# The mLSTM value projection taken two panels at a time, with 512 moving weight columns

## The chip, the cores and the metric

One core of a Trainium2 chip runs the whole kernel. The metric is the device time of one execution in microseconds (us); the median of three runs of the kernel before is 1903.33 us (1903.31 to 1904.78). All arithmetic is in float32; the large matrix products are made of three products of values rounded to fp32r (see below), so that a product of two float32 matrices costs three passes of TensorE.

## The reference, cut to what matters

Two layers of a parallel-branch block over 256 latent tokens and 256 context tokens, D_MODEL 1024. Per layer:

```
h = adaLN(RMSNorm(x))
parts = h @ w_in          # mLSTM q, k, v, o-gate, gates; GQA q, k, v; conv u, B, C; 3 merge gates
mlstm: 4 heads, q and k 128 wide, v 256 wide, both directions, context state first
    num = sum_s (q k^T * w_intra) v + ... ; den = row sum of the same weights
    h_out = num / max(|den|, exp(-m))
ym = h_out * rsqrt(mean h_out^2) * gain * sigmoid(o)
merged = sum_b sigmoid(gate_b) * (y_b @ P_b);   x += g1 * (merged @ w_out)
x += g2 * (relu(adaLN(RMSNorm(x)) @ w_up)^2 @ w_down)
```

The change concerns `v`, the third part: for 512 tokens and 4 heads of 256 columns it is h (512 x 1024) times 1024 columns of w_in.

## The kernel before, in words

**Panels.** All weights are cut into panels of 1024 rows and 256 columns (1 MB each). A layer has 90 of them, numbered through both layers by p; in layer 0 the panels 0 and 1 are mLSTM k (mk), 2 and 3 are q (mq), 4 to 7 are v (mv, one panel for each head, c = 0 to 3), 8 to 11 are the o-gate (mo). Layer 1 has the same at 90 and up, so its value panels are 94 to 97. A panel goes through these steps:
- SyncE loads it by one DMA into a buffer of `raw`, which has RAW = 4 places, place p % 4 (`load_panel`, L902). The load waits until panel p - 4 has been multiplied (L939).
- ScalarE rounds it to fp32r into `wH` (L1297, two instructions of 128x1024), which has HIGH = 3 places, place p % 3. It waits until panel p - 3 has been multiplied (L1295), because that panel's weights lie in the same place.
- VectorE subtracts: `wL` = raw - wH (L1697, two instructions), written over the raw values.
- TensorE multiplies (`run_panel`) and adds three products for each tile of 128 rows of the contraction (8 tiles, kt): high x high, high x low and low x high. Its last matmul increments the semaphore panel_done.
- ScalarE or VectorE takes the result out of one of the two PSUM slots (p % 2), and slot_free allows panel p + 2.

Two panels ahead: in the step of panel p, ScalarE and VectorE first split panel p + 2 (AHEAD = 2), and only then take the result of panel p out.

**Order of the work.** `make_plan` writes one list of steps, and each engine walks through it in order and does its own part of each step; semaphores join the engines. Around the value panels the list says: mq 1, gate_scan (VectorE), mv 0, gate_e, mv 1, gate_e2, mv 2, gate_cols (32 small transposing matmuls on TensorE, L1149), mv 3, then for head 0: weigh (TensorE L1162 and L1169, ScalarE exponentials L1512 into EP, VectorE L2011, GpSimd's triangular mask L1658), the o-gate panel mo 0 on TensorE beside that, and value (TensorE L1193), which needs the mask, the products and the head's values in `vaug`.

**The value panels.** For most panels the weights are the stationary operand and 512 tokens (256 in layer 1 where only latent tokens count) are the moving one. For the mv panels it is the other way round, as the result must have the tokens on the partitions: 128 tokens of h are loaded as the stationary operand and the 256 columns of the panel's weights move. So each mv panel has 4 token tiles x 8 kt x 3 products = 96 matmuls with 256 moving columns (L986 to L988). VectorE copies the result into `vaug` (L1753), and `mv_ready` counts one for each panel; value of head h waits for h + 1 of the layer.

Of the kernel before, what the change touches and what calls it, by code (L numbers as in the profile page):

```python
# [20 lines left out]
F32 = mybir.dt.float32  # L21
# [5 lines left out]
P = 128  # L27
# [505 lines left out]
def trunk(nc, x, c, ctx_in, c_ctx, w_ada, b_ada, norm1, norm2, w_in, gate_b, mnorm, qnorm, knorm, conv_w,  # L533
          w_pm, w_pa, w_pc, w_out, w_up, w_down, fnorm, consts, out):
    ctx = ExitStack()
    with ctx:
# [8 lines left out]
        xT = at("xT", [P, KT, TOK], F32, o); o += K16  # L545
        hH = at("hH", [P, KT, TOK], F32R, o); o += K16
        hL = at("hL", [P, KT, TOK], F32R, o); o += K16
        raw = at("raw", [P, RAW, KT, PC], F32, o); o += RAW * KT * PC * 4
        wL = at("wL", [P, RAW, KT, PC], F32R, o - RAW * KT * PC * 4)
        wH = at("wH", [P, HIGH, KT, PC], F32R, o); o += HIGH * KT * PC * 4  # L550
# [294 lines left out]
        def next_panel(st):  # L845
            p = st["p"] + AHEAD
            return PANELS[p] if p < NPANELS else None

        def raw_arrived(eng, p):
            eng.wait_ge(s_raw[p % RAW], 16 * (p // RAW + 1))  # L850

# [15 lines left out]
        @block.sync  # L867
        def _(sp):
            def load_ada(a):
                q = ADA[a]  # L870
                home = q["home"]
                if same_home[a]:
                    ada_finished(sp, same_home[a][-1])
                if a >= FILL_N2[0]:
                    l = 0 if a < FILL_N2[1] else 1
                    if home[0] == "W":
                        sp.wait_ge(acc_ready, len(PAIRS))
                        sp.wait_ge(y_ready, y_no[1, "a", NC - 1] + 1)
                    elif home[0] == "Y":
                        sp.wait_ge(panel_done, panel_no("proj", l, NC - 1, 2) + 1)  # L880
                    else:
                        sp.wait_ge(panel_done, panel_no("up", 0, NC - 1, FF // D - 1) + 1)
                at_ = (q["m"] * NC + q["c"]) * PC
                sp.dma_start(ada_w[home][:, :, :], w_ada[q["l"]].rearrange("(k p) n -> p k n", p=P)[:, :, at_:at_ + PC]  # L884
                             ).then_inc(s_ada[home], 16)

            def load_pair(n):
                q = PAIRS[n]
                if same_pair[n]:
                    sp.wait_ge(acc_ready, same_pair[n][-1] + 1)  # L890
                if n == 0:
                    sp.wait_ge(y_ready, y_no[0, "a", NC - 1] + 1)
                elif n == FIRST_PAIRS:
                    sp.wait_ge(h_ready, h_no[0, "m", NC - 1] + 1)
                elif n == FIRST_PAIRS + 1:
                    sp.wait_ge(h_ready, h_no[0, 2] + KT)
                at_ = (q["m"] * NC + 2 * q["j"]) * PC
                sp.dma_start(pair_w[q["home"]][:, :, :], w_ada[q["l"]].rearrange("(k p) n -> p k n", p=P)[:, :, at_:at_ + 2 * PC]
                             ).then_inc(s_pair[q["home"]], 16)

            def load_panel(p):
                sp.dma_start(raw[:, p % RAW, :, :], panel_source(PANELS[p])).then_inc(s_raw[p % RAW], 16)  # L902
# [12 lines left out]
            load_panel(1)  # L915
            sp.dma_start(con[:, FIRST_COLS:CONST_COLS], consts[:, FIRST_COLS:CONST_COLS]).then_inc(s_tables, 16)
            for st in PLAN:
                if st["k"] == "panel" and (st["kind"], st["c"]) == ("mk", 0):

                    l = st["l"]  # L920
                    if l:
                        sp.wait_ge(wg_ready, l)
                        sp.wait_ge(gc_ready, l)
                    sp.dma_start(w_gate[:, :, :], w_in[l].rearrange("(k p) n -> p k n", p=P)[
                        :, :, COL["mg"]:COL["mg"] + 16]).then_inc(s_wg, 16)
                    for g in range(2):
                        for dr in range(2):
                            sp.dma_start(gb[dr * 4:dr * 4 + 4, g:g + 1],
                                         gate_b[l, dr, g].rearrange("(h a) -> h a", a=1)).then_inc(s_wg, 16)
                if st["k"] == "pairload":  # L930
                    load_pair(st["n"])
                elif st["k"] == "adaload":
                    load_ada(st["a"])
                if st["k"] != "panel":
                    continue
                p = st["p"]
                if p >= 2:
                    if p >= RAW:
                        sp.wait_ge(panel_done, p - RAW + 1)  # L939
                    load_panel(p)  # L940
            ov = out[0].rearrange("(t p) d -> p t d", p=P)
            for tt in range(2):
                sp.wait_ge(fa_ready, tt + 1)
                sp.wait_ge(f_ready, tt + 1)
                sp.dma_start(ov[:, tt, :], f_out[:, tt, :]).then_inc(s_out, 16)
            sp.wait_ge(s_out, 32)

        @block.tensor
        def _(pe):
# [12 lines left out]
            def run_panel(st, kts=slice(0, KT)):  # L962
# [15 lines left out]
                if kind in ("mv", "av"):  # L978
                    pe.wait_ge(ready, need(KT - 1))
                    split_ready(0)  # L980
                    split_ready(KH)
                    for tt in range(TT):
                        dst = pp[:, slot, tt // 2, (tt % 2) * PC:(tt % 2 + 1) * PC]
                        ts_ = slice(tt * P, (tt + 1) * P)
                        for kt in range(KT):
                            pe.matmul(dst, hi[:, kt, ts_], wH[:, hs_, kt, :], start=kt == 0, stop=False)  # L986
                            pe.matmul(dst, hi[:, kt, ts_], wL[:, ls_, kt, :], start=False, stop=False)  # L987
                            last = pe.matmul(dst, lo[:, kt, ts_], wH[:, hs_, kt, :], start=False, stop=kt == KT - 1)  # L988
                    last.then_inc(panel_done, 1)
                    return  # L990
                ts_ = slice(0, TOK) if kind in ("mk", "ak") else cols(l)
                seen = 0
                for kt in range(KT)[kts]:
                    split_ready(kt)
                    dsts = [pp[:, slot, b, ts_] for b in range(NB)]
                    wh = [wH[:, hs_, kt, b * P:(b + 1) * P] for b in range(NB)]
                    wl = [wL[:, ls_, kt, b * P:(b + 1) * P] for b in range(NB)]
                    first, end = kt == 0, kt == KT - 1
                    if need(kt) > seen:

# [17 lines left out]
            for st in PLAN:  # L1018
# [161 lines left out]
                elif k == "value":  # L1180
# [107 lines left out]
        def _(act):  # L1288
            def split(st):
# [2 lines left out]
                raw_arrived(act, p)  # L1292
                if p >= HIGH:

                    act.wait_ge(panel_done, p - HIGH + 1)  # L1295
                for a in (0, KH):
                    act.activation(wH[:, p % HIGH, a:a + KH, :], raw[:, p % RAW, a:a + KH, :], ACT.Copy).then_inc(wH_ready, 1)  # L1297

            def y_high(no, src, kts, ts_):

# [272 lines left out]
        def _(pool):  # L1573
# [8 lines left out]
            def first_rest():  # L1582

                for i in range(2):
                    ks = slice(i * KH, (i + 1) * KH)
                    pool.wait_ge(wH_ready, i + 1)
                    pool.tensor_tensor(wL[:, 0, ks, :], raw[:, 0, ks, :], wH[:, 0, ks, :].bitcast(F32),
                                       ALU.subtract).then_inc(wL0_ready, 1)

            def y_rest(no, src, kts, ts_):  # L1590
# [84 lines left out]
        def _(dve):  # L1675
# [15 lines left out]
            def split(st):  # L1691

                p = st["p"]
                for i in range(2):
                    ks = slice(i * KH, (i + 1) * KH)
                    dve.wait_ge(wH_ready, 2 * p + i + 1)
                    dve.tensor_tensor(wL[:, p % RAW, ks, :], raw[:, p % RAW, ks, :], wH[:, p % HIGH, ks, :].bitcast(F32),  # L1697
                                      ALU.subtract).then_inc(wL_ready, 1)

            n_norm = n_half = n_nt = 0  # L1700
            for st in PLAN:
# [39 lines left out]
                elif k == "panel":  # L1741
# [6 lines left out]
                    src = pp[:, slot, :, ts_]  # L1748
                    if kind in ("mv", "av"):
                        dve.wait_ge(panel_done, p + 1)  # L1750
                        dst = vaug[:, :, c_, 0:MV] if kind == "mv" else v_a[:, :, :]
                        done = mv_ready if kind == "mv" else av_ready
                        dve.tensor_copy(dst, pp[:, slot, :, :].rearrange("p b (t n) -> p (b t) n", t=2)).then_inc(done, 1)  # L1753
# [421 lines left out]
```

## Time and profile before

| | |
|---|---|
| median of three runs | 1903.33 us (1903.31 to 1904.78) |
| the profiled execution | 1904.54 us, its span 1902.5 us |
| TensorE busy | 97% of the span, mean granted clock 0.989 of full |
| VectorE, ScalarE, GpSimd busy | 56%, 36%, 8% |
| chain that ended last | TensorE 91%, VectorE 4% |

The span is the time from the first to the last instruction that the profiler shows; 2.0 us of the execution lie outside it. Matmuls overlap in TensorE's pipeline, so a matmul's own duration (0.28 us for 256 moving columns, 0.39 for 512) is longer than the distance from one start to the next; it is the distance of starts that adds up to time. The granted clock is 1.0 where TensorE may run at 2.4 GHz and 0.5 where it is held at 1.2 GHz.

### The profile page before, as it was taken

To read this page: it belongs to the slowest core of one execution; us is meant where nothing else is said; L and a number is where in the kernel's file an instruction comes from. 1 tells how busy PE (TensorE), PEld (TensorE's weight loads), DVE (VectorE), ACT (ScalarE), POOL (GpSimd) and SP (SyncE) were. 2 spreads that over 40 slices of the span, in tenths; PEclk is the share of its full clock that TensorE was granted. 3 is DMA by queue.
4 is the path that set the end of the run, shared out by engine and by line. 5 is a ranking of instruction groups with operands and counts; after the bars stand their busy time and mean duration, and the time that the engine had idled before them with its cause. 6 is when DMAs were issued, how large, how long until landed. Compare 5 with 4: busy or idle time off the path is not lost.

```text
span 1902.5 us, 26175 instructions
## 1 busy us (share of the span) xinstructions
PE 1854.5 (97%) x10845; PEld 1598.2 (84%) x10845; DVE 1062.7 (56%) x1562; ACT 690.4 (36%) x946; POOL 158.2 (8%) x158
## 2 busy tenths in 40 slices
PE   6999999999999999989999999899999999999998
PEld 4797788888888888867888888699998899989997
DVE  5535643545556666467565554644646656566664
ACT  3423543333222222343232223333544434444443
POOL 2101100001110111220000000200100110120000
PEclk9999999999999999999999999999999999999999
DMA  9221122211443453624443525232242365555552
GB/s 322 69 87 45 45 89 67 67 61 51 133 147 119 151 191 101 221 95 149 133 136 130 199 89 180 66 110 70 65 132 89 111 222 181 190 184 180 188 187 89
DMA packets 226293, 244.56 MB, mean 129 GB/s; under 512 B 5796, under 2 KB 210944, under 8 KB 226176
## 3 DMA queue, kind: packets, MB, share of 16 engines
q1 hardware_dynamic: 225872, 242.80, 39.8%
q8 instruction: 86, 1.41, 0.3%
q14 instruction: 31, 0.25, 0.0%
q10 hardware_dynamic: 304, 0.10, 0.0%
HBM read 241.84 MB, written 1.05 MB: 128 GB/s over the span
## 4 chain that ended last, share of the span: by engine, by line
PE 91%; DVE 4%; ACT 1%; SPq 1%; issue 1%; DMA 1%; POOL 0%; DVEq 0%; ACTq 0%
PE pp L1004 20%; PE pp L1008 20%; PE pp L1005 19%; PE pp L1013 5%; PE pp L1011 5%; PE pp L1012 5%; PE pc L1193 3%; PE pp L986 2%; PE pp L987 2%; PE pp L988 2%; PE pc L1245 1%; PE pc L1283 1%; SPq L884 1%; PE pc L1260 1%; DMA raw<-in_w_in 1%
## 5 line engine op out<-in xcount | busy, mean ns | idle before, releaser
L1004 PE MATMUL pp<-hH,wH 128*128 128x512 f32 (+1 forms) x1760 | 590.9, 346 | 4.4 <-ACT hH L1482 4.4
L1005 PE MATMUL pp<-hH,wL 128*128 128x512 f32 (+1 forms) x1760 | 581.3, 341 | 0.0
L1697 DVE TENSOR_TENSOR wL<-raw,wH 128x1024 fp32r<-128x1024 f32 x358 | 448.6, 1294 | 203.3 <-ACT wH L1297 200.1
L1297 ACT ACTIVATE wH<-raw 128x1024 fp32r<-128x1024 f32 x360 | 360.4, 1050 | 356.1 <-PE pp L1013 173.9
L1008 PE MATMUL pp<-hL,wH 128*128 128x512 f32 (+1 forms) x1760 | 456.4, 341 | 2.6 <-POOL hL L1635 1.9
L1004 PEld LDWEIGHTS pp<-hH,wH 128*128 128x128 f32 x1760 | 335.2, 190 | 50.7 <-issue 14.8
L1005 PEld LDWEIGHTS pp<-hH,wL 128*128 128x128 f32 x1760 | 335.1, 190 | 37.6 <-issue 1.7
L1008 PEld LDWEIGHTS pp<-hL,wH 128*128 128x128 f32 x1760 | 304.3, 190 | 43.8 <-POOL hL L1635 6.8
L1011 PE MATMUL pp<-yH,wH 128*128 128x512 f32 (+1 forms) x448 | 150.8, 337 | 0.0
L1012 PE MATMUL pp<-yL,wH 128*128 128x512 f32 (+1 forms) x448 | 150.6, 336 | 0.0
L1013 PE MATMUL pp<-yH,wL 128*128 128x512 f32 (+1 forms) x448 | 150.6, 336 | 0.0
L1004 PE MATMUL pp<-yH,wH 128*128 128x512 f32 (+1 forms) x448 | 149.3, 344 | 0.0
L1005 PE MATMUL pp<-yH,wL 128*128 128x512 f32 (+1 forms) x448 | 146.0, 337 | 0.0
L1008 PE MATMUL pp<-yL,wH 128*128 128x512 f32 (+1 forms) x448 | 114.1, 336 | 0.0
L1818 DVE SCALAR_TENSOR_TENSOR xT<-pp,modT,xT 128x256 f32<-128x256 f32 x120 | 50.7, 478 | 98.9 <-PE pp L1013 98.8
L1870 DVE SCALAR_TENSOR_TENSOR acc<-pair_W,c_wide,acc 128x512 f32<-128x512 f32 x126 | 102.2, 848 | 3.8 <-DVE xT L1818 1.2
L1004 PEld LDWEIGHTS pp<-yH,wH 128*128 128x128 f32 x448 | 85.3, 190 | 10.9 <-issue 2.4
L1005 PEld LDWEIGHTS pp<-yH,wL 128*128 128x128 f32 x448 | 85.2, 190 | 9.4 <-issue 0.7
L1013 PEld LDWEIGHTS pp<-yH,wL 128*128 128x128 f32 x448 | 85.2, 190 | 8.7
L986 PE MATMUL pp<-wH,hH 128*128 128x256 f32 x320 | 92.5, 289 | 0.0
L1012 PEld LDWEIGHTS pp<-yL,wH 128*128 128x128 f32 x448 | 85.1, 190 | 8.7
L1011 PEld LDWEIGHTS pp<-yH,wH 128*128 128x128 f32 x448 | 85.1, 190 | 8.8
(235 smaller groups left out, 2076.6 us busy)
## 6 DMA issues: line engine op xcount, KB each, us to landing
raw<-in_w_in SPq DMA_DIRECT2D x84, 1024.0 KB, 5.2
raw<-in_w_up SPq DMA_DIRECT2D x32, 1024.0 KB, 5.6
raw<-in_w_down SPq DMA_DIRECT2D x32, 1024.0 KB, 5.2
pair_W<-in_w_ada SPq DMA_DIRECT2D x10, 2048.0 KB, 7.9
ada_Y<-in_w_ada SPq DMA_DIRECT2D x10, 1024.0 KB, 11.9
ada_H<-in_w_ada SPq DMA_DIRECT2D x8, 1024.0 KB, 11.9
raw<-in_w_proj_m SPq DMA_DIRECT2D x8, 1024.0 KB, 5.3
raw<-in_w_proj_a SPq DMA_DIRECT2D x8, 1024.0 KB, 5.4
```

Of the source, the lines that this page charges most:

```text
L986: pe.matmul(dst, hi[:, kt, ts_], wH[:, hs_, kt, :], start=kt == 0, stop=False)
L1004: pe.matmul(dsts[b], wh[b], hi[:, kt, ts_], start=first, stop=False)
L1005: pe.matmul(dsts[b], wl[b], hi[:, kt, ts_], start=False, stop=False)
L1008: last = pe.matmul(dsts[b], wh[b], lo[:, kt, ts_], start=False, stop=end)
L1011: pe.matmul(dsts[b], wh[b], hi[:, kt, ts_], start=first, stop=False)
L1012: pe.matmul(dsts[b], wh[b], lo[:, kt, ts_], start=False, stop=False)
L1013: last = pe.matmul(dsts[b], wl[b], hi[:, kt, ts_], start=False, stop=end)
L1193: last = pe.matmul(b[:, 0:MV + 1], EP[:, d, off:off + P], vaug[:, s, h, :], start=i == 0, stop=i == len(terms) - 1)
L1297: act.activation(wH[:, p % HIGH, a:a + KH, :], raw[:, p % RAW, a:a + KH, :], ACT.Copy).then_inc(wH_ready, 1)
L1697: dve.tensor_tensor(wL[:, p % RAW, ks, :], raw[:, p % RAW, ks, :], wH[:, p % HIGH, ks, :].bitcast(F32), ALU.subtract).then_inc(wL_ready, 1)
L1818: i = dve.scalar_tensor_tensor(out=xT[:, kt, hs], in0=pp[:, slot, b, hs], scalar=modT[:, l, g + kt, v:v + 1], in1=xT[:, kt, hs], op0=ALU.m ...
L1870: i = dve.scalar_tensor_tensor(out=acc[:, v, :], in0=src[:, kt, :], scalar=c2[:, kt, v:v + 1], in1=acc[:, v, :], op0=ALU.mult, op1=ALU.add)
```

## The change

The buffers `raw`, `wL` and `wH` are laid out [k-tile, place, column] in place of [place, k-tile, column]: two panels in neighbouring places then give, for one k-tile, 512 contiguous columns. The load, the rounding and the subtraction use the new index order; they have the same instructions of the same shapes in elements.

The mv panels are taken in pairs (c = 0 and 1, c = 2 and 3). Each of the two run_panel calls of a pair now does two of the four token tiles for both heads, so 2 x 8 x 3 = 48 matmuls with 512 moving columns. Before the first matmul TensorE waits until both panels of the pair are split. As the second call reads the first panel's weights too, whoever overwrites the first panel's place (the load of the panel 4 later, the rounding of the panel 3 later) waits for one panel more: `shared(p)` is 1 for the first panel of a pair. The copy into `vaug` writes two token tiles of two heads, and the value of head h waits for both calls of its pair. The av panel keeps its form.

```
-        raw = at("raw", [P, RAW, KT, PC], F32, o); o += RAW * KT * PC * 4
+        raw = at("raw", [P, KT, RAW, PC], F32, o); o += RAW * KT * PC * 4
...
+        def shared(p):
+            return int(PANELS[p]["kind"] == "mv" and PANELS[p]["c"] % 2 == 0)
...
-                        sp.wait_ge(panel_done, p - RAW + 1)
+                        sp.wait_ge(panel_done, p - RAW + 1 + shared(p - RAW))
...
+                if kind == "mv":
+                    c = st["c"]
+                    p0 = p - c % 2
+                    h0, l0 = p0 % HIGH, p0 % RAW
+                    assert h0 < HIGH - 1 and l0 < RAW - 1
+                    pe.wait_ge(ready, need(KT - 1))
+                    pe.wait_ge(wL_ready, 2 * (p0 + 1))
+                    for i in range(2):
+                        tt = 2 * (c % 2) + i
+                        dst, ts_ = pp[:, slot, i, :], slice(tt * P, (tt + 1) * P)
+                        for kt in range(KT):
+                            pe.matmul(dst, hi[:, kt, ts_], wH[:, kt, h0:h0 + 2, :], start=kt == 0, stop=False)
+                            pe.matmul(dst, hi[:, kt, ts_], wL[:, kt, l0:l0 + 2, :], start=False, stop=False)
+                            last = pe.matmul(dst, lo[:, kt, ts_], wH[:, kt, h0:h0 + 2, :], start=False, stop=kt == KT - 1)
+                    last.then_inc(panel_done, 1)
+                    return
...
-                    pe.wait_ge(mv_ready, MH * l + h + 1)
+                    pe.wait_ge(mv_ready, MH * l + h // 2 * 2 + 2)
...
-                    act.wait_ge(panel_done, p - HIGH + 1)
+                    act.wait_ge(panel_done, p - HIGH + 1 + shared(p - HIGH))
...
-                        dst = vaug[:, :, c_, 0:MV] if kind == "mv" else v_a[:, :, :]
+                        t0, h0 = 2 * (c_ % 2), c_ // 2 * 2
+                        dst = vaug[:, t0:t0 + 2, h0:h0 + 2, 0:MV] if kind == "mv" else v_a[:, :, :]
```

## Rows read from the trace of the kernel before

**Rows 1.** The page: busy time of the engines, and the chain that ended last.
```profile
PE 1854.5 (97%) x10845; PEld 1598.2 (84%) x10845; DVE 1062.7 (56%) x1562; ACT 690.4 (36%) x946; POOL 158.2 (8%) x158
...
PE 91%; DVE 4%; ACT 1%; SPq 1%; issue 1%; DMA 1%; POOL 0%; DVEq 0%; ACTq 0%
```
**Rows 2.** Waits of TensorE: waiter, releaser, total us, times, longest us.
```profile
PE pc L1058 <- DVE n_sum L1902: 11.9, 4, 4.2
...
PE pc L1068 <- DVE small L1908: 0.2, 1, 0.2
```
**Rows 3.** Timeline of TensorE, layer 0: start us, us, instruction.
```profile
62.22 0.40 PE L1131 MATMUL pc<-hH,wg 128*128 128x512 f32 x1
...
65.95 0.39 PE L1004 MATMUL pp<-hH,wH 128*128 128x512 f32 x1
...
88.56 0.62 PE L1008 MATMUL pp<-hL,wH 128*128 128x512 f32 x2
...
92.64 0.62 PE L1008 MATMUL pp<-hL,wH 128*128 128x512 f32 x2
93.09 0.28 PE L986 MATMUL pp<-wH,hH 128*128 128x256 f32 x1
...
104.61 0.28 PE L986 MATMUL pp<-wH,hH 128*128 128x256 f32 x1
```
**Rows 4.** Timelines of ScalarE and VectorE, layer 0, with idle time before and releaser.
```profile
84.66 1.99 ACT L1297 ACTIVATE wH<-raw 128x1024 fp32r<-128x1024 f32 x2
...
93.29 1.03 ACT L1341 ACTIVATE qk<-pp 128x1024 f32<-128x1024 f32 x1 [6.65 <-PE pp L1008]
...
85.73 2.36 DVE L1697 TENSOR_TENSOR wL<-raw,wH 128x1024 fp32r<-128x1024 f32 x2 [3.58 <-ACT wH L1297]
```
**Rows 5.** Timelines of four engines in layer 1, from weigh to value of head 0.
```profile
1305.68 0.50 PE L1162 MATMUL pc<-M_parts,one_row 40*128 40x256 f32 x2
...
1306.28 2.81 ACT L1512 ACTIVATE EP<-pc,g_col 128x256 f32<-128x256 f32 x8 [15.27 <-PE pc L1162]
...
1309.18 2.48 DVE L2011 TENSOR_TENSOR EP<-EP,pc 128x256 f32<-128x256 f32 x8 [2.17 <-ACT EP L1512]
...
1311.87 2.99 POOL L1658 TENSOR_SCALAR_AFFINE_SELECT EP<-EP 128x128 f32<-128x128 f32 x4 [83.73 <-DVEq L2019]
...
1314.97 5.22 PE L1193 MATMUL pc<-vaug,EP 128*128 128x257 f32 x23 [1.12 <-issue]
```
**Rows 6.** Timelines of VectorE and TensorE in layer 1, start of the value panels.
```profile
1253.56 2.36 DVE L1697 TENSOR_TENSOR wL<-raw,wH 128x1024 fp32r<-128x1024 f32 x2 [3.59 <-ACT wH L1297]
...
1254.19 0.28 PE L986 MATMUL pp<-wH,hH 128*128 128x256 f32 x1
```
**Rows 7.** The same place in layer 0: GpSimd's mask and TensorE's value.
```profile
152.44 2.00 POOL L1658 TENSOR_SCALAR_AFFINE_SELECT EP<-EP 128x128 f32<-128x128 f32 x8 [94.12 <-DVEq L2019]
...
156.19 7.53 PE L1193 MATMUL pc<-vaug,EP 128*128 128x257 f32 x34
```
**Rows 8.** Windows of TensorE: stretch, us, busy us, granted clock, DMA share, GB/s.
```profile
17.40:21.64 4.24, 0.00 (x0) 1.00 1.10 349
22.60:26.00 3.40, 3.16 (x23) 0.50 1.10 348
...
1431.20:1433.70 2.50, 0.01 (x1) 1.00 0.84 251
1435.80:1439.00 3.20, 3.20 (x7) 0.50 0.00 0
1890.00:1895.00 5.00, 2.26 (x20) 1.00 0.00 0
1896.60:1902.40 5.80, 1.00 (x4) 0.50 0.45 181
...
131.40:144.59 13.19, 13.19 (x98) 0.87 0.07 25
```
**Rows 9.** The page's DMA issues: tile, KB each, median us from issue to landing.
```profile
raw<-in_w_in SPq DMA_DIRECT2D x84, 1024.0 KB, 5.2
```

More of the change, by code:

```diff
@@ L547, in trunk @@
         hL = at("hL", [P, KT, TOK], F32R, o); o += K16
-        raw = at("raw", [P, RAW, KT, PC], F32, o); o += RAW * KT * PC * 4
-        wL = at("wL", [P, RAW, KT, PC], F32R, o - RAW * KT * PC * 4)
-        wH = at("wH", [P, HIGH, KT, PC], F32R, o); o += HIGH * KT * PC * 4
+        raw = at("raw", [P, KT, RAW, PC], F32, o); o += RAW * KT * PC * 4
+        wL = at("wL", [P, KT, RAW, PC], F32R, o - RAW * KT * PC * 4)
+        wH = at("wH", [P, KT, HIGH, PC], F32R, o); o += HIGH * KT * PC * 4
         Y = o
@@ L901, in load_panel @@
             def load_panel(p):
-                sp.dma_start(raw[:, p % RAW, :, :], panel_source(PANELS[p])).then_inc(s_raw[p % RAW], 16)
+                sp.dma_start(raw[:, :, p % RAW, :], panel_source(PANELS[p])).then_inc(s_raw[p % RAW], 16)
             sp.dma_start(con[:, 0:FIRST_COLS], consts[:, 0:FIRST_COLS]).then_inc(s_small, 16)
@@ L977, in run_panel @@
                 hi, lo, ready, need = operand(st)
-                if kind in ("mv", "av"):
+                if kind == "mv":
[14 more added lines that the diff above has]
+                    return
+                if kind == "av":
                     pe.wait_ge(ready, need(KT - 1))
@@ L985, in run_panel @@
                         for kt in range(KT):
-                            pe.matmul(dst, hi[:, kt, ts_], wH[:, hs_, kt, :], start=kt == 0, stop=False)
-                            pe.matmul(dst, hi[:, kt, ts_], wL[:, ls_, kt, :], start=False, stop=False)
-                            last = pe.matmul(dst, lo[:, kt, ts_], wH[:, hs_, kt, :], start=False, stop=kt == KT - 1)
+                            pe.matmul(dst, hi[:, kt, ts_], wH[:, kt, hs_, :], start=kt == 0, stop=False)
+                            pe.matmul(dst, hi[:, kt, ts_], wL[:, kt, ls_, :], start=False, stop=False)
+                            last = pe.matmul(dst, lo[:, kt, ts_], wH[:, kt, hs_, :], start=False, stop=kt == KT - 1)
                     last.then_inc(panel_done, 1)
@@ L995, in run_panel @@
                     dsts = [pp[:, slot, b, ts_] for b in range(NB)]
-                    wh = [wH[:, hs_, kt, b * P:(b + 1) * P] for b in range(NB)]
-                    wl = [wL[:, ls_, kt, b * P:(b + 1) * P] for b in range(NB)]
+                    wh = [wH[:, kt, hs_, b * P:(b + 1) * P] for b in range(NB)]
+                    wl = [wL[:, kt, ls_, b * P:(b + 1) * P] for b in range(NB)]
                     first, end = kt == 0, kt == KT - 1
@@ L1293, in split @@
                 if p >= HIGH:
[L1295 removed]
+                    act.wait_ge(panel_done, p - HIGH + 1 + shared(p - HIGH))
                 for a in (0, KH):
[L1297 removed]
+                    act.activation(wH[:, a:a + KH, p % HIGH, :], raw[:, a:a + KH, p % RAW, :], ACT.Copy).then_inc(wH_ready, 1)
             def y_high(no, src, kts, ts_):
@@ L1586, in first_rest @@
                     pool.wait_ge(wH_ready, i + 1)
-                    pool.tensor_tensor(wL[:, 0, ks, :], raw[:, 0, ks, :], wH[:, 0, ks, :].bitcast(F32),
+                    pool.tensor_tensor(wL[:, ks, 0, :], raw[:, ks, 0, :], wH[:, ks, 0, :].bitcast(F32),
                                        ALU.subtract).then_inc(wL0_ready, 1)
@@ L1696, in split @@
                     dve.wait_ge(wH_ready, 2 * p + i + 1)
-                    dve.tensor_tensor(wL[:, p % RAW, ks, :], raw[:, p % RAW, ks, :], wH[:, p % HIGH, ks, :].bitcast(F32),
+                    dve.tensor_tensor(wL[:, ks, p % RAW, :], raw[:, ks, p % RAW, :], wH[:, ks, p % HIGH, :].bitcast(F32),
                                       ALU.subtract).then_inc(wL_ready, 1)
@@ L1750, in _ @@
                         dve.wait_ge(panel_done, p + 1)
-                        dst = vaug[:, :, c_, 0:MV] if kind == "mv" else v_a[:, :, :]
+                        t0, h0 = 2 * (c_ % 2), c_ // 2 * 2
+                        dst = vaug[:, t0:t0 + 2, h0:h0 + 2, 0:MV] if kind == "mv" else v_a[:, :, :]
                         done = mv_ready if kind == "mv" else av_ready
-                        dve.tensor_copy(dst, pp[:, slot, :, :].rearrange("p b (t n) -> p (b t) n", t=2)).then_inc(done, 1)
+                        src = pp[:, slot, :, :].rearrange("p b (t n) -> p b t n" if kind == "mv" else "p b (t n) -> p (b t) n", t=2)
+                        dve.tensor_copy(dst, src).then_inc(done, 1)
                         dve.wait_ge(done, MH * l + c_ + 1 if kind == "mv" else l + 1)
```

## The prediction

> **What bounds the kernel now.** I read the page's busy line and chain first. TensorE is busy 97% of the span and holds 91% of the chain that ended last [rows 1]. So a microsecond that TensorE gains or loses is a microsecond of the result, and work of the other engines counts only where TensorE has to wait for it. Next I read TensorE's waits. The longest group is a norm, 11.9 us in 4 waits, and the list goes down to 0.2 us without any wait for the split weights (DVE wL) or for a weight DMA [rows 2]. The split is therefore always early now. The change alters both sides: matmuls of the value panels, and who waits for a split. I followed the second through the timelines of the three engines, panel by panel, with the plan beside them.
>
> **Part 1: the matmuls.** Between the starts of mv 0 and mv 1 lie 96 matmuls of 256 columns, from 93.09 to 104.61 [rows 3]: 11.52 us, 0.1200 us each. Matmuls with 512 moving columns: from 88.56 to 92.64 lie 18 of them [rows 3], 0.2267 us each. A pair of 256 takes 0.2400, so one of 512 in its place saves 0.0133 us. Eight panels with 96 matmuls become 384 of 512 columns: 384 x 0.0133 = 5.1 us gained. There is a second row for 512 columns: the 16 matmuls of the gate weights, which all add into one PSUM bank as the new ones will, start at 62.22 and are followed by the next at 65.95 [rows 3], 0.2331 each; by that the gain is 384 x 0.0069 = 2.6 us. But they have a semaphore wait before every second one, which neither the panels nor the new ones have; I take 5.1 and keep 2.6 as the poor end. For a better end no row speaks.
>
> The Trainium skill bears on this: TensorE: Matmul & The Clock Gate, section "Back-to-back issue gap", gives N / 2.4 + 2.5 ns between isolated matmuls at full clock, and says itself that this leaves the weight load out. By it a wider matmul would save only the 2.5 ns, about 1 us over 384, as an estimate from that page. The trace disagrees for this stream: 120 and 227 ns are 13 and 14 ns above N / 2.4.
>
> **Part 2: the second pair waits for a place in wH.** wH has three places. In layer 0 the first pair, panels 4 and 5, lies in places 1 and 2, panel 6 goes to place 0 and panel 7 to place 1, which is panel 4's. Before, panel 7 could be rounded when panel 4 was done, a whole panel (11.5 us) ahead of panel 6's start. Now the second call still reads panel 4's weights, so ScalarE waits until panel 5 is done; but TensorE's next work is the pair 6 and 7, and it waits for both splits. Nothing stands between on TensorE (gate_e2 has no matmul, gate_cols comes after mv 2). So the whole split of panel 7 is bare. Its price, counted from the moment when the next matmul would have started: ScalarE starts 0.20 us after it (93.29 against 93.09 [rows 3, 4]); from its start to the end of VectorE's second half it is 85.73 + 2.36 - 84.66 = 3.43 us [rows 4], with both engines free as they would be here (ScalarE is waiting in order at this very instruction, VectorE too); TensorE starts 0.11 us after its releaser (1314.97 after GpSimd's end at 1311.87 + 2.99 = 1314.86 [rows 5]); the first matmul after a pause is some 0.1 us slower. Together 3.8 us. In layer 1 it is the same (94 in place 1, 95 in 2, 96 in 0, 97 in 1). Two layers: 7.6 us lost. As bounds, 3.4 each if the transitions cost nothing, 4.1 if the strided pieces of 256 columns make each of the four instructions a little slower; for that no row speaks, and the same number of elements moves.
>
> Queued behind the waiting instruction: on VectorE, the copy of panel 5 into vaug and gate_e2, needed by panel 7's slot and by gate_cols, both an entire panel later; on ScalarE the split of panel 8. Both are hidden by panel 6, 10.9 us of matmuls. Without that cover they would cost their own 1.2 and some 3 us.
>
> **Part 3: the first pair in layer 1.** TensorE now needs panel 95 split before 94 begins. In layer 0 the split of panel 5 ends at 88.09, 5.0 us before 93.09: hidden [rows 3, 4]. In layer 1 the mq panels have only the latent columns and are half as long; VectorE ends the split of 95 at 1253.56 + 2.36 = 1255.92, and mv 0 starts at 1254.19 [rows 6]. It would start at 1256.03, and with the slower first matmul 1.9 us are lost.
>
> **Part 4: the split of panel 9 (99) moves to a tight place.** Panel 9 takes place 0, panel 6's; its rounding now waits for the end of panel 7 instead of panel 6. In ScalarE's order it stands before the exponentials of weigh, head 0. Now, in layer 1, the exponentials start 0.6 us after TensorE has left the value panels (1306.28, where weigh's first matmul starts at 1305.68 [rows 5]). After the change the rounding comes first: 0.2 until it starts and 2.0 for itself [rows 4], so they start 2.2 us after that moment, 1.6 later. VectorE has its split and the vaug copy in this time too (3.6 + 1.2 us after the end), and is free before the exponentials end at 5.1. Then everything of the head's chain moves by 1.6: products, mask, value. In layer 1 TensorE already idles 1.12 us, until the mask is done [rows 5], so the 1.6 is lost in full. In layer 0 the mask ends at 154.44 and TensorE gets to value at 156.19, busy until then [rows 7]: 1.75 us of slack cover the 1.6, and I charge 0.1. If that slack were gone it would cost 1.6 more.
>
> **Part 5: the clock.** TensorE ran at half clock after each pause of 2.5 us or more: there are six of them behind the first 15 us, the first of 4.24 us, the shortest of 2.50, the last of 2.74 (5.00 less 2.26 busy), and each is followed by a stretch at 0.50 [rows 8]. Half clock costs half of its stretch: mv 3 in layer 0, of which the first part ran at 0.50, took 13.19 us instead of 11.52 [rows 8], 1.7 more. The bare splits of part 2 are pauses of 3.8 us, so I expect the same after them; part of the slow stretch may fall into the pause itself, so I take 1.3 for each instead of 1.7, 2.6 together. The pause in layer 1 before value grows from 1.12 to 2.7 us; there I take 0.4, since part of it would be hidden or missed. Bounds: nothing at all, and 1.7 for each of the three, 5.1.
>
> **Part 6: what costs nothing.** Layout: the same instructions and element counts; a weight load reads 128 neighbouring columns as before, and the source rows of a panel are 1 KB, so the DMA moves the same 1 KB pieces. Loads of panels 8 and 10 start one panel later, but land 5.2 us after issue [rows 9], with at least a panel before they are needed. If this cover were gone, ScalarE would wait up to 5 us for each. The copy into vaug has 1024 elements a partition as before, beside the next panel.
>
> **The sum**, against the profiled execution of 1904.54 us: -5.1 + 7.6 + 1.9 + 1.6 + 0.1 + 2.6 + 0.4 = +9.1, so 1913.6 us. That execution is 1.2 above the median; on the median of 1903.33 it is 1912.4, rounded 1912.5.
>
> **Rivals.**
> (a) The pauses cost no clock. For it: all six of the pauses stand beside short or small matmuls (the norm, the attention), which is not so here, where full matmuls end just before the pause and begin just after it. Against it: six of six, two of them shorter than 3.8 us by a third. Then +6.1: 1909.4 us.
> (b) The gain of part 1 is only 2.6 (accumulation into one bank as in the gate matmuls): +11.6, 1914.9 us.
> (c) Faster: the bare split doesn't exist, because ScalarE and VectorE get panel 7 done beside panel 5. This would need that its release is earlier than the end of panel 5, from which everything turns: if the wait is met half a panel (5.4 us) earlier, part 2 and its clock are gone, and -5.1 + 1.9 + 1.6 + 0.1 + 0.4 = -1.1 remains; with parts 3 and 4 hidden as well it is -5.1, 1898.2 us. Against it: the wait counts whole panels, and panel_done is raised by the last matmul.
> (d) The change doesn't do what it says: a matmul of 512 columns takes as long as two of 256, because its moving operand comes from the weight buffers, to which ScalarE and VectorE write at the same time. Then the gain is 0: +14.2, 1917.5 us. Nothing in the rows shows such an effect on TensorE.
>
> **How the numbers follow.** The forecast 0.58, (a) 0.20, (b) 0.08, (d) 0.03, (c) 0.08 (half of it at -5.1, half around -1.1), the rest is unnamed. The measurement can tell from no change what is over about 0.2%, 3.8 us. Faster by more: 0.05, from (c); within: 0.06, from (c) and from a stall smaller than I count; slower: 0.89. The range goes from 1906.5 (the case (a) with parts 3 and 4 mostly absorbed) to 1916 (b, with the full price of the clock).
>
> **What would show it.** In the profile after: 48 matmuls from L986's successor at 0.227 us distance; in TensorE's waits two of about 3.5 us with DVE wL as releaser, and one of 1.8 in layer 1 at the start of mv 0; before the value of head 0 in layer 1 an idle time of 2.7 in place of 1.12; a stretch at 0.5 behind each 3.8 us pause. The forecast is wrong if no wait for wL shows, or if the first pair's second panel is split before it is needed in layer 1.

## The result: 9.3 us slower, the matmuls faster as counted and TensorE waiting for splits

The changed kernel takes 1912.90 us (median of four runs, 1912.81 to 1916.92) against 1903.61 for the kernel before: a ratio of 1.0053, 95% interval 1.0035 to 1.0070. The forecast was 1912.5. In a second session it was 1913.03 (five runs) against 1905.56 (sixteen), 1.0043 (1.0029 to 1.0056). The ratios weigh all runs of a kernel and are not the ratios of the two medians, so the two can differ by about 0.05%.

The page of the changed kernel, its busy line and the chain that ended last, answers to [rows 1]:

```profile
PE 1853.2 (97%) x10461; PEld 1578.6 (83%) x10461; DVE 1060.3 (55%) x1562; ACT 690.2 (36%) x946; POOL 158.2 (8%) x158
...
PE 90%; DVE 4%; ACT 2%; SPq 1%; issue 1%; DMA 1%; POOL 0%; DVEq 0%; ACTq 0%; POOLq 0%
```

There are 384 matmuls fewer, and yet TensorE's busy time falls by only 1.3 us. What the wide matmuls save, 5.1 us by the distances below, is mostly taken back by half clock: span times one less the mean granted clock is some 4 us more than before (1910.8 x 0.013 against 1902.5 x 0.011, an estimate). The waits of TensorE say more, beside [rows 2] (waiter, releaser, total us, times, longest us):

```profile
PE pc L1079 <- DVE n_sum L1925: 11.9, 4, 4.3
PE pp L994 <- DVE wL L1718: 9.1, 3, 3.7
...
PE pc L1214 <- issue: 2.7, 1, 2.7
```

The second line is new: three waits of value matmuls for a split, 9.1 us. The last is the pause before the value of head 0 in layer 1, 1.12 us before. TensorE's timeline shows them one by one (start us, us, instruction, idle time before it and releaser); the first four lines are the first pair in layer 0 and the bare split behind it, then the starts of both pairs in layer 1, then the value of head 0:

```profile
91.61 0.39 PE L994 MATMUL pp<-wH,hH 128*128 128x512 f32 x1
...
113.14 0.39 PE L996 MATMUL pp<-wH,hL 128*128 128x512 f32 x1
117.22 0.47 PE L994 MATMUL pp<-wH,hH 128*128 128x512 f32 x1 [3.69 <-DVE wL L1718]
...
1258.53 0.47 PE L994 MATMUL pp<-wH,hH 128*128 128x512 f32 x1 [1.72 <-DVE wL L1718]
...
1284.26 0.76 PE L994 MATMUL pp<-wH,hH 128*128 128x512 f32 x1 [3.69 <-DVE wL L1718]
...
1323.43 0.58 PE L1214 MATMUL pc<-vaug,EP 128*128 128x257 f32 x1 [2.69 <-issue]
```

From 91.61 to 113.14 there are 95 distances of starts: 0.2266 us each. The first bare split, on ScalarE and then on VectorE, with the copy into vaug queued behind it, and further down the late split of panel 99 ahead of the exponentials:

```profile
113.62 2.00 ACT L1318 ACTIVATE wH<-raw 128x1024 fp32r<-128x1024 f32 x2 [15.62 <-PE pp L996]
...
1312.73 2.00 ACT L1318 ACTIVATE wH<-raw 128x1024 fp32r<-128x1024 f32 x2 [24.88 <-PE pp L996]
1314.64 2.79 ACT L1533 ACTIVATE EP<-pc,g_col 128x256 f32<-128x256 f32 x8
```
```profile
114.71 2.36 DVE L1718 TENSOR_TENSOR wL<-raw,wH 128x1024 fp32r<-128x1024 f32 x2 [10.80 <-ACT wH L1318]
116.99 1.22 DVE L1776 COPY vaug<-pp 128x1024 f32<-128x1024 f32 x1
```

The granted clock behind these pauses (windows of TensorE: stretch, us, busy us, clock, DMA share, GB/s):

```profile
113.50:117.20 3.70, 0.03 (x1) 1.00 0.68 204
118.80:122.10 3.30, 3.30 (x10) 0.50 0.74 232
...
1280.60:1282.60 2.00, 0.00 (x0) 1.00 0.33 59
1282.70:1284.20 1.50, 0.00 (x0) 0.50 1.08 386
1284.30:1289.40 5.10, 5.10 (x12) 0.50 0.84 264
1320.80:1323.40 2.60, 0.00 (x0) 1.00 0.53 140
1323.70:1327.00 3.30, 3.30 (x9) 0.50 0.50 175
```

Laid beside each other by the starts of the same instructions, the two profiled executions differ as follows (us; a stretch with half clock in it is marked h; gate_sel is a step of small matmuls for the gates, one projection panel ahead of mv 0):

| stretch | layer 0 before | after | layer 1 before | after |
|---|---|---|---|---|
| gate_sel to mv 0 | 16.14 h | 14.59 | 9.38 | 11.26 |
| mv 0, 1, 2 | 34.64 | 38.30 h | 34.65 | 39.27 h |
| gate_cols | 3.67 | 4.70 h | 3.77 h | 3.66 |
| mv 3 | 13.19 h | 13.24 h | 13.07 h | 11.11 |
| weigh to value, head 0 | 11.60 | 11.61 | 9.29 | 10.86 |
| value, head 0, to the next weigh | 12.07 | 12.07 | 6.23 | 7.92 h |
| sum | 91.31 | 94.51 | 76.39 | 84.08 |

These stretches lose 10.9 us, and the rest of the span wins 2.6, where two half-clock stretches of the kernel before, one of the attention at 1435.7 us and one of a norm at 1701.9, are missing after. The spans differ by 8.3. This is one execution of each kernel, and half clock falls differently in each. The pause of 2.5 us ahead of the attention's stretch [rows 8] is as long in the changed kernel, but nothing at half clock follows it there:

```profile
1441.40:1443.80 2.40, 0.00 (x0) 1.00 0.86 255
1444.00:1450.00 6.00, 6.00 (x38) 1.00 0.18 63
```

### The profile page after: what moved, and what is told of

It reads as the page before. It is cut to its first block, busy times and chain, and to the rows that moved or that the text cites. A ratio compares the mean times of both kernels' runs of the same rounds, so it can differ in the third digit from the quotient of the medians.

```text
span 1910.8 us, 25399 instructions
## 1 busy us (share of the span) xinstructions
PE 1853.2 (97%) x10461; PEld 1578.6 (83%) x10461; DVE 1060.3 (55%) x1562; ACT 690.2 (36%) x946; POOL 158.2 (8%) x158
## 4 chain that ended last, share of the span: by engine, by line
PE 90%; DVE 4%; ACT 2%; SPq 1%; issue 1%; DMA 1%; POOL 0%; DVEq 0%; ACTq 0%; POOLq 0%
PE pp L1025 19%; PE pp L1029 19%; PE pp L1026 19%; PE pp L1034 5%; PE pp L1032 5%; PE pp L1033 5%; PE pc L1214 3%; PE pp L994 2%; PE pp L995 2%; PE pp L996 2%; PE pc L1304 1%; PE pc L1266 1%; SPq L888 1%; DVE wL L1718 1%; PE pc L1281 1%
## 5 line engine op out<-in xcount | busy, mean ns | idle before, releaser
L1718 DVE TENSOR_TENSOR wL<-raw,wH 128x1024 fp32r<-128x1024 f32 x358 | 448.6, 1294 | 248.5 <-ACT wH L1318 245.9
L1025 PEld LDWEIGHTS pp<-yH,wH 128*128 128x128 f32 x448 | 85.0, 190 | 10.9 <-issue 2.4
L1033 PEld LDWEIGHTS pp<-yL,wH 128*128 128x128 f32 x448 | 85.0, 190 | 8.8
L1029 PEld LDWEIGHTS pp<-yL,wH 128*128 128x128 f32 x448 | 77.0, 190 | 8.8
```

The costliest lines, as they stand in the source:

```text
L1025: pe.matmul(dsts[b], wh[b], hi[:, kt, ts_], start=first, stop=False)
L1029: last = pe.matmul(dsts[b], wh[b], lo[:, kt, ts_], start=False, stop=end)
L1033: pe.matmul(dsts[b], wh[b], lo[:, kt, ts_], start=False, stop=False)
L1718: dve.tensor_tensor(wL[:, ks, p % RAW, :], raw[:, ks, p % RAW, :], wH[:, ks, p % HIGH, :].bitcast(F32), ALU.subtract).then_inc(wL_ready, 1)
```

## The experiments

The time of one kernel scatters from run to run, because the half-clock stretches fall differently. So each table entry has the ratio to the kernel before from the same session, and a second number: the mean, over the runs, of span times mean granted clock. It is the span with half of each half-clock stretch taken out, and so nearly free of that scatter. It is too low by half of the time in which TensorE idled at half clock. Its standard error is 0.1 to 0.9 us, 1.5 for the pairs of 256 (four runs). For the runs of the kernel before beside the first measurement no clocks are on record but one, so the first line of the table takes the 1879.3 of the next session.

| kernel | us, median | ratio to before (95%) | span x clock, difference to before |
|---|---|---|---|
| changed | 1912.90 | 1.0053 (1.0035 to 1.0070) | +7.2 |
| changed again | 1913.03 | 1.0043 (1.0029 to 1.0056) | +7.4 |
| layout only | 1905.09 | 1.0006 (0.9996 to 1.0015) | 0.0 |
| pairs, 256 wide | 1918.32 | 1.0075 (1.0060 to 1.0090) | +11.9 |
| first pair only | 1900.62 | 0.9984 (0.9972 to 0.9997) | +0.1 |
| second pair only | 1906.38 | 1.0007 (0.9992 to 1.0021) | +0.9 |
| pauses filled | 1910.17 | 1.0024 (1.0014 to 1.0033) | +6.7 |
| splits moved | 1917.00 | 1.0056 (1.0035 to 1.0076) | +3.7 |
| covered | 1906.74 | 1.0003 (0.9993 to 1.0014) | -1.5 |
| mask first | 1899.06 | 0.9965 (0.9952 to 0.9977) | -4.6 |
| before, mask first | 1904.02 | 0.9990 (0.9981 to 0.9999) | -1.0 |
| columns between | 1901.43 | 0.9974 (0.9962 to 0.9985) | +0.2 |

The kernel before had medians of 1904.03 (first four of the experiments), 1905.35 (the next three) and 1905.56 (the last four); its span x clock was 1879.3, 1878.9 and 1879.0.

### Layout only

The buffers in the new order, everything else as before: `shared` returns 0, the mv branch of run_panel, the mv_ready wait and the copy are those of the kernel before.

> Only the new buffer layout; matmuls, waits and copies as in the kernel before. Theory A (all of the +9.3 us comes from the pairing: bare splits, a late exponential, and clock): no change, within 1 us of the kernel before; ScalarE's rounding stays at 1.05 us an instruction, VectorE's subtraction at 1.22, the panel DMA at 5.2 us to landing. Rival B (the strided buffers cost something at 720 instructions and 180 loads, which shows on the chain): slower by 2 to 9 us.

No change: 1.0006 (0.9996 to 1.0015), +0.0 in span x clock. The groups by line, with the mean in ns:

```profile
L1701 DVE TENSOR_TENSOR wL<-raw,wH 128x1024 fp32r<-128x1024 f32 x358 | 448.2, 1293 | 204.1 <-ACT wH L1301 200.9 <-DVE xT L1822 0.2 <-DVE EP L2015 0.2
...
L1301 ACT ACTIVATE wH<-raw 128x1024 fp32r<-128x1024 f32 x360 | 360.3, 1049 | 359.3 <-PE pp L1017 177.3 <-DMA raw<-in_w_in 53.3 <-DMA raw<-in_w_up 46.3
```

Before they were 1294 and 1050 ns. Landing stays at 5.2 us. The layout is free, and rival B falls.

### The pairs with 256 wide matmuls

```
-                        for kt in range(KT):
-                            pe.matmul(dst, hi[:, kt, ts_], wH[:, kt, h0:h0 + 2, :], start=kt == 0, stop=False)
+                        for g in range(2):
+                            half = dst[:, g * PC:(g + 1) * PC]
+                            for kt in range(KT):
+                                pe.matmul(half, hi[:, kt, ts_], wH[:, kt, h0 + g, :], start=kt == 0, stop=False)
...
```

> The changed kernel with all its waits and the same division of the pair's work, but each 512 wide matmul as two of 256 columns. Theory A (a 512 wide matmul saves 0.0133 us against two of 256, 384 of them): 5.1 us slower than the changed kernel, +14.4 us on the kernel before, give or take 1.7 for each half-clock stretch that falls otherwise. Rival C (the gain was only 2.6 us and the pauses cost less than counted): +11.9. Rival D (no gain from 512 columns): as the changed kernel, +9.3.

1918.32 us, 14.3 above the kernel before, and 5.3 to 5.4 above the changed kernel's two medians; 4.7 by span x clock; taken against the kernel before of each session it is 5.0 and 6.8. Its trace has the same three waits for wL, 9.1 us. That the gain isn't nothing is clear from the times. They don't exclude a gain of 2.6: the interval above is 11 to 17 us on the kernel before, and rival C's 11.9 lies in it. The distances of starts decide that. The first value panel of this kernel starts and ends with

```profile
91.59 0.28 PE L996 MATMUL pp<-wH,hH 128*128 128x256 f32 x1
...
102.98 0.28 PE L998 MATMUL pp<-wH,hL 128*128 128x256 f32 x1
```

which is 95 distances of 0.1199 us, so two of 256 take 0.240 where one of 512 takes 0.2266 in the changed kernel: 5.1 us over 384.

### One pair alone

A function `paired(c)` chooses which heads are taken as a pair: `c < 2` in the one kernel, `c >= 2` in the other. The rest goes the old way.

> Only heads 0 and 1 are taken as a pair, heads 2 and 3 as before. The place of panel 4 is still freed only after panel 5, but panel 6 doesn't need panel 7's split, so this split is covered by panel 6. Theory A: -2.6 us from the matmuls, +1.9 for the pause at the start of the value panels in layer 1, no pause in the middle: -0.7 us on the kernel before, within 2 us of it. Rival E (what costs is the paired reading itself, or the longer waits of the loads): half of the change's loss, +4 to +5 us.

> Only heads 2 and 3 are taken as a pair. Panel 7's split waits for panel 4 as before and is done beside panel 5. What remains is the late split of panel 9 (99) ahead of the exponentials. Theory A: -2.6 us from the matmuls, +1.6 in layer 1 and +0.1 in layer 0 before the value of head 0, up to 1.7 of clock after the pause of 2.7 us: -0.9 to +0.8 us on the kernel before. Rival E (the pairing itself costs): +4 to +5 us.

With the first pair only, 1900.62 (0.9984), 3.4 us below the kernel before and so outside the 2 us around -0.7 that were expected; span x clock is +0.1, so the gain over before is clock and not work. Its waits in layer 1, from gate_sel to the value of head 0, contain the pause at the start and no bare split:

```profile
PE pp L998 <- DVE wL L1722: 1.7, 1, 1.7
PE pc L1218 <- issue: 1.1, 1, 1.1
```

mv 0 to 2 take 33.36 us in layer 0, 1.28 less than 34.64: the gain of two heads, paid by nothing. With the second pair only, the one wait left in this stretch of layer 1 is that before value:

```profile
PE pc L1218 <- issue: 2.7, 1, 2.7
```

Its time is that of the kernel before within what can be told (1.0007, 0.9992 to 1.0021; the medians are 2.4 us apart). Half of the change costs next to nothing, whichever half; the whole costs 7.5 to 9.3. That points to the place in wH that the two pairs pass on to each other. Rival E falls. Span x clock is +0.9 where -0.9 was expected at full clock; where the difference lies stays open.

### The pauses filled

```
+                    for _ in range({(0, 2): 16, (1, 0): 8, (1, 2): 16}.get((l, c), 0)):
+                        pe.matmul(pp[:, slot, 0, :], hi[:, 0, 0:P], hi[:, 0, :], start=True, stop=True)
                     pe.wait_ge(wL_ready, 2 * (p0 + 1))
...
+                    if l == DEPTH - 1 and h == 0:
+                        q = panel_no("mo", l, 1)
+                        pe.wait_ge(slot_free[q % 2], q // 2)
+                        for _ in range(11):
+                            pe.matmul(pp[:, q % 2, 0, :], hH[:, 0, 0:P], hH[:, 0, :], start=True, stop=True)
```

> The changed kernel with unused matmuls of 512 columns laid into its three new pauses (16 in each middle pause, 8 at the start of the value panels in layer 1, 11 before the value of head 0 in layer 1), writing to PSUM that the next panel overwrites. They end before the wait does, or up to 0.3 us after it, so no pause gets shorter: what goes is only the idle array. Theory A (the clock falls because of the pauses, 2 to 3 us of the loss are clock): no stretch at 0.50 behind the three places, 2 to 4 us faster than the changed kernel, +5.5 to +7.5 us on the kernel before. Rival F (the clock's falls are elsewhere or chance, the loss is pauses and nothing else): the same as the changed kernel, +9.3, or up to 0.5 slower.

1910.17 us, 1.0024 (1.0014 to 1.0033) against 1.0053 and 1.0043: 4.8 us above the kernel before, a little under the 5.5 to 7.5 expected, where the changed kernel is 9.3 and 7.5 above it. So 2.7 to 4.5 us are gone, by work that nobody needs. Span x clock stays at +6.7. The same places as above, in this kernel:

```profile
113.00:117.00 4.00, 4.00 (x19) 1.00 0.56 161
118.00:122.00 4.00, 4.00 (x19) 1.00 0.85 268
1279.50:1283.50 4.00, 4.00 (x20) 1.00 0.08 12
1284.00:1288.00 4.00, 4.00 (x18) 1.00 1.09 368
1320.00:1323.00 3.00, 3.00 (x19) 1.00 0.40 95
1323.60:1327.00 3.40, 3.23 (x15) 1.00 0.64 223
```

Full clock at all of them, and mv 0 to 2 take 36.63 and 36.72 us in place of 38.30 and 39.27: 34.64 less three times 0.64 for the wide matmuls, plus the 3.9 of the pause, which is now filled but no shorter. So the pauses themselves took the clock, and rival F falls.

### Two splits moved

On ScalarE and VectorE the split of panel 5 (95) comes ahead of gate_exp and gate_sel, and that of panel 9 (99) behind the exponentials and the products of head 0:

```
+        def split_here(st):
+            if st["k"] == "gate_exp":
+                return PANELS[panel_no("mv", st["l"], 1)]
+            if st["k"] == "weigh" and st["h"] == 0:
+                return PANELS[panel_no("mo", st["l"], 1)]
...
                 elif k == "gate_exp":
+                    split(split_here(st))
...
+                    if h == 0:
+                        split(split_here(st))
```

> The changed kernel with two splits moved in the order of ScalarE and VectorE: that of the first pair's second panel (5, 95) ahead of the gates' arithmetic, and that of panel 9 (99) behind the exponentials and products of head 0. Theory A: the pause at the start of the value panels in layer 1 (1.7 us in the trace) goes, that before the value of head 0 in layer 1 shrinks from 2.7 to about 1.1; the two pauses of 3.7 us in the middle stay. 3.4 us faster than the changed kernel, up to 1.7 more with the clock: +4 to +6 us on the kernel before. Rival G (these two places are covered otherwise, and the loss is the middle pauses alone): within 1 us of the changed kernel, +8.5 to +9.5.

The expectation failed in its time: 1917.00 us, no better than the changed kernel. In the trace the stretch to mv 0 in layer 1 is back at 9.38 us, as before, and the middle pauses stay; of TensorE's waits:

```profile
PE pp L1005 <- DVE wL L1732: 7.4, 2, 3.7
```

But weigh to value in layer 1 takes 10.27 us, not 9.29. The mask of GpSimd is what grew, and this kernel shows why (GpSimd, then VectorE beside it):

```profile
1318.43 3.98 POOL L1693 TENSOR_SCALAR_AFFINE_SELECT EP<-EP 128x128 f32<-128x128 f32 x4 [89.55 <-DVEq L2057]
```
```profile
1318.45 5.04 DVE L1732 TENSOR_TENSOR wL<-raw,wH 128x1024 fp32r<-128x1024 f32 x4 [0.23 <-DVE EP L2049]
```

Four mask instructions take 3.98 us beside four subtractions, 2.99 beside two [rows 5]. Span x clock is +3.7, 3.6 less than the changed kernel, near the 3.4 expected. The rest is clock: its mean granted clock is 0.984 over six runs, where the changed kernel has 0.987. Only part of that has a name (the pause of 2.1 us before value still cost a half-clock stretch); why the other stretches fell so badly in four of six runs stays open.

### Covered

On top of that, the first call of the second pair does panel 6 alone first:

```
+                    if c == 2:
+                        for g in range(2):
+                            pe.wait_ge(wL_ready, 2 * (p0 + g))
+                            for i in range(2):
+                                half, ts_ = pp[:, slot, i, g * PC:(g + 1) * PC], slice(i * P, (i + 1) * P)
...
```

> As the kernel with the two splits moved, and the first call of the second pair (panels 6 and 7) in 256 wide matmuls, 48 on panel 6 first, 5.8 us, and only then 48 on panel 7, so that panel 7's bare split of 3.7 us is covered. The other three calls of the four keep 512 columns. Theory A: no new pause is left, 3/4 of the matmul gain remains: -3.8 us on the kernel before, 1899.8 (-0.20%), give or take 1.7 for a half-clock stretch. Rival H (the middle pauses come from something else than the wait for panel 7's split, such as PSUM slots or loads): the pauses stay, +4 to +6.

No wait for wL is left, in either layer, and mv 0 to 2 take 33.36 and 33.39 us: the cause of the middle pauses is the wait for panel 7's split, and rival H falls. The time is 1906.74, 1.0003 (0.9993 to 1.0014), not the 0.9980 expected. Two errors of mine: the longer mask (+1.0 us in layer 1, +0.3 in layer 0), and the half clock behind its pause of 2.1 us, value of head 0 again 7.93 us in place of 6.23.

### The mask first

```
                     if h == 0:
+                        dve.wait_ge(mask_ready, l * MH + 1)
                         split(split_here(st))
```

and in the other kernel the same wait alone, put into the kernel before ahead of the split in the step of mo 0.

> The covered version (two splits moved, second pair's first call in 256 columns), and VectorE waits for GpSimd's mask of head 0 before it goes on with the splits of panels 9 and 10 (99 and 100). Theory J (GpSimd's four mask instructions take 3.98 us there only because VectorE's subtractions run beside them; alone they take 1.13): in layer 1 the mask ends 2.9 us earlier, the pause of 2.1 us before the value of head 0 goes altogether and with it the half-clock stretch behind it: 2 to 4 us faster than the covered version; with three quarters of the matmul gain and the 1.1 us of the kernel before's own pause -5 us on the kernel before, 1899 to 1901. Rival K (the mask takes as long as it takes at this place): no faster than the covered version, or 1 us slower.

> The kernel before with only that wait for the mask, in front of VectorE's split in the step of the first o-gate panel. Theory J: the mask of head 0 in layer 1 takes 1.1 us in place of 2.99, the pause of 1.12 us before its value goes: -1.1 us (and nothing of the clock, since behind 1.12 us it did not fall). Rival K: no change or 1 us slower.

```profile
1309.03 1.02 POOL L1704 TENSOR_SCALAR_AFFINE_SELECT EP<-EP 128x128 f32<-128x128 f32 x4 [83.01 <-DVEq L2068]
```

The same four instructions take 1.02 us with VectorE held back. TensorE's pause is gone, weigh to value is 8.01 us in layer 1. The full version takes 1899.06 us, 0.9965 (0.9952 to 0.9977): it beats the kernel before by 6.5 us and the changed one by 14. Against the covered version it is 7.7 us by the medians of the two sessions, where 2 to 4 were expected; 3.1 of them are work by span x clock, the rest is clock, of which the gone stretch behind the pause explains 1.7. In the kernel before the wait alone gives 0.9990 (0.9981 to 0.9999), with -1.0 in span x clock, as expected. The Trainium skill has the rule: SBUF — State Buffer, "SBUF: two separate sides", says that VectorE and GpSimd share a pair of ports under an exclusive lock, which a VectorE instruction with two SBUF inputs holds against a reading GpSimd instruction until it ends. The subtraction has two such inputs, and 1.02 against 2.99 and 3.98 us agree with it. So do the single instructions: with VectorE held back each of the four takes 0.29 us, and beside the subtractions two of four (three of four in the kernel with the splits moved) take 1.27 to 1.28, about as long as a subtraction.

### gate_cols between the matmuls

On top of the version with the mask first, the 16 small transposing matmuls (32 records in the trace, two for each) are issued inside mv 3, two after every third of its first 24 wide matmuls:

```
+                            for _, (name, t_, c0) in list(zip(range(2), small_ones)):
+                                one = pe.matmul(gb_[:, c0:c0 + 8], rows[name][0:8, t_ * P:(t_ + 1) * P], ident[0:8, 0:8],
+                                                start=True, stop=True)
```

> As the version with the mask first, and the 16 small transposing matmuls of gate_cols, which stand as a block of 3.67 us ahead of the fourth value panel, are laid between that panel's first 48 matmuls, two after every third. Theory L (the clock falls behind this block because it does little in the array; in every profile so far but one of a layer it was followed by half clock, at 1.6 us or more): no half-clock stretch in or behind the fourth value panel, 2 to 5 us faster than the version with the mask first, 1895 to 1898. Rival M (the small matmuls cost more between others than in a block, or the clock falls anyway): no faster.

Both theories are half right. In the profiled execution, the fastest of the six, the half-clock stretches at both places are gone (windows of TensorE with the columns as above; granted clock 1.00), and the mean clock rises from 0.988 to 0.990:

```profile
118.00:144.00 26.00, 26.00 (x145) 1.00 0.16 48
1280.00:1300.00 20.00, 20.00 (x111) 1.00 0.01 2
```

But the work got longer by 4.8 us in span x clock: one round of three wide and two small matmuls takes 133.45 - 132.02 = 1.43 us,

```profile
132.02 0.50 PE L1023 MATMUL pp<-wH,hH 128*128 128x512 f32 x1
132.35 0.39 PE L1024 MATMUL pp<-wL,hH 128*128 128x512 f32 x1
132.58 0.40 PE L1025 MATMUL pp<-wH,hL 128*128 128x512 f32 x1
132.91 0.61 PE L1027 MATMUL pc<-con,e_run 8*128 8x8 f32 x4
133.45 0.50 PE L1023 MATMUL pp<-wH,hH 128*128 128x512 f32 x1
```

against 0.68 for three wide ones and 0.46 for two small ones in the block (3.67 / 16 each): 0.29 more, 8 times in each of two layers. 1901.43 us is no gain on 1899.06: here rival M is right in the time. What the expectation says of earlier profiles was too strong: of 24 such blocks in the twelve profiles without this edit, 20 had half clock in or behind them; the other four all stood behind a pause of 3.7 us.

### The changed kernel again

> The changed kernel once more, on the same chip as the versions beside it, with more rounds. Theory A: +9.3 us on the kernel before (1.0049), of which about 6 us stand in the trace at full clock and the rest is clock. If its first measurement was helped or hurt by how the half-clock stretches fell, +6 to +12.

+7.5 us by the medians, 1.0043, within what was expected; the first measurement stands. Its profile again has half clock behind both bare splits (117.9 and 1285.3 us) and before head 0's value.

## Why the prediction was right, step by step

- **Part 1, the matmuls.** 5.1 us: the distance of starts is 0.2266 us in the trace (0.2267 taken), and the kernel with 256 wide matmuls in the same pairs has 0.1199 and is 4.7 to 6.8 slower, depending on what is compared. Their accumulation into one bank left the distance at 0.2266, not the 0.2331 of the gate matmuls, so 2.6 was too careful an end.
- **Part 2, the bare split.** 3.8 us for each. From the last matmul's start, 113.14, to the next, 117.22, less one distance of 0.23: 3.85; ScalarE, VectorE and the order of the copy behind it stand in the trace as written. The covered kernel shows the cause.
- **Part 3, the start in layer 1.** 1.9 forecast, 9.38 to 11.26 = 1.88 measured; gone when the split is moved.
- **Part 4, the late split of 99.** 1.6 forecast in layer 1, 9.29 to 10.86 = 1.57 measured; in layer 0 0.1 forecast, 0.01 measured: the slack held.
- Full clock together: +6.1 forecast. Measured in the stretches: 2 x 3.85 + 1.88 + 1.57 + 0.01 - 5.1 = +6.1. By span x clock over all runs it is 7.2 and 7.4; the rest of 1.1 to 1.3 us has no place in the profile.
- **Part 5, the clock.** The mechanism was right for the three new pauses and the sizes off in both directions. Layer 0's pause cost 38.30 - 36.63 = 1.67, layer 1's 39.27 - 36.72 = 2.55, that before value 7.92 - 6.23 = 1.69: 5.9 in this profile, where I had 3.0. I took 0.4 for the pause of 2.7 us and should have charged it in full: in all six profiles with a pause of 2.1 to 2.7 us at this place (the changed kernel twice, pairs 256 wide, second pair only, splits moved, covered) a half-clock stretch followed. On the other side, half clock that the kernel before had elsewhere was absent after: 8.3 - 6.1 - 5.9 = -3.7 us in this profile, of which the stretch at gate_sel in layer 0 (-1.55) and mv 3 in layer 1 (-1.3 beyond its 0.64) are in the table. By the filled kernel, the clock of the three pauses is worth 2.7 to 4.5 us of the time. So the total came out right partly because two errors in the clock cancel, which was luck.
- **What part 5 left out.** The slow stretch that gave the price of 1.7 us, mv 3 in layer 0, stood behind no pause. Of the ten half-clock stretches behind the first 15 us of the kernel before, six follow the six pauses of 2.5 us or more and four do not (80.6, 131.8, 1292.3 and 1701.9 us); the forecast says nothing of these, and three of the four are absent after. Nor does the rule of six in six hold elsewhere: the pause of 2.50 us in layer 1's attention, one of the six, is in all thirteen profiles and had half clock in or behind it in eight; in both profiles of the changed kernel it had none.
- **Part 6, layout and loads at nothing.** Shown for the layout. The loads of panels 8 and 10 did arrive later (ScalarE waits 3.21 us for raw, at 118.83), and hid behind panel 6 as said.
- **The rivals.** (a), no clock, is refuted by the windows and by the filled kernel, (d) by the time of the 256 wide pairs, (b) by the distances of starts, (c) by the waits.
- **The range.** Its upper end was added up wrongly: (b) with the full price of the clock is 11.6 + 5.1 - 3.0 = 13.7, so 1917 and not 1916. The measured time lies below either.

## What to carry to other kernels

Taking two buffers as one also frees them as one: before doing it, walk the ring of places and find whose turn falls on the place that is now held longer; with three places and two pairs in a row the next split had no cover at all, while one pair alone cost next to nothing. A pause of TensorE has to be priced with the half-clock stretch behind it: here pauses of 2.1 us and more mostly had one, but not all, so it belongs in the sum with a chance and not as certain. And once the waits are known, the cheap mends are in the order of the other engines: the two moved splits, one half-wide first call and one wait turned +7.5 us into -6.5 in the same session.

## What the runs showed of the hardware that was not expected

- GpSimd's four mask instructions took 1.02 us alone, 2.99 beside two of VectorE's subtractions and 3.98 beside four. The 1.12 us pause of the kernel before was nothing but this: with the wait for the mask alone it is gone.
- A pause of 1.7 us (start of the value panels in layer 1, four profiles) never brought half clock, those of 3.7 us in the middle of the value panels and of 2.1 to 2.7 us before the value of head 0 did in all fourteen cases. But length doesn't decide alone: the pause of 2.50 us in layer 1's attention did in 8 of 13 profiles, and one of 1.31 us at a norm (1698.7 us before) in 5 of 13. A block of small matmuls that kept TensorE busy for 3.67 us did in 20 of 24.
- Small matmuls of 8x8 cost 0.23 us each in a block and 0.37 each between wide ones.
- The same kernel scatters by up to 14 us (second pair only: 1897.5 to 1911.1) in runs whose mean clock is 0.985 to 0.992; span times clock scatters by a fraction of it.
